# GpSimd builds the next state-space tile's tables between a pair's two tiles, ahead of the next tile's parameters

## What is computed

```
for i in range(DEPTH):                          # DEPTH 2, SEQ 256, D_MODEL 2048
    h = rmsnorm(x, norm_w[i])
    (u, s5_gate, z, xbc, dt_raw, q, k, v, att_gate,
     merge_logits) = jnp.split(h @ w_in[i], pts, axis=-1)
    y_s5  = s5_mixer(u, ...) * silu(s5_gate)        # diagonal complex state-space model
    y_ssd = ssd_mixer(z, xbc, dt_raw, ...)          # Mamba-2, 16 heads, chunks of 64
    y_att = window_attention(q, k, v, att_gate, ...)# 16 heads, window 128
    branches = einsum('bnw,nwd->bnd', [y_s5, y_ssd, y_att], w_branch[i])
    x = x + (sum_b sigmoid(merge_logits_b) * branches_b) @ w_out[i]
```

## Time and profile before

| | us |
|---|---|
| median of 3 runs | 1879.06 (1876.44 to 1883.75) |
| the profiled execution, its own time | 1878.58 |
| its span | 1876.9 |
| PE busy | 1826.9 (97%) |
| DVE busy | 1384.8 (74%) |
| ACT busy | 951.5 (51%) |
| POOL busy | 541.5 (29%) |

### The profile page before, as it was taken

One profiled execution on the slowest core, in us unless ns is written; L12 is line 12 of the kernel. 1 busy time (PEld: TensorE's weight loads), 2 busy tenths in 40 slices (PEclk: granted clock), 3 DMA queues, 4 the chain that ended last, 5 costly groups with the idle time before them and its releaser, 6 DMA issues.

```text
span 1876.9 us, 34933 instructions
## 1 busy us (share of the span) xinstructions
PE 1826.9 (97%) x11720; PEld 1555.7 (83%) x11720; DVE 1384.8 (74%) x1865; ACT 951.5 (51%) x1128; POOL 541.5 (29%) x632
## 2 busy tenths in 40 slices
PE   6999999999999999999999999999999999999998
PEld 5888888878787888888889888887777788888887
DVE  6986666888787777666588766678787876766656
ACT  5344444666657564434454344456656565533334
POOL 5053444163451010003412434433352600000044
PEclk9999999999999999999999999999999999999999
DMA  7455555556555547665555555555565555566655
GB/s 286 160 203 185 185 193 186 189 201 215 185 188 189 182 175 265 224 240 210 201 188 188 191 184 193 185 200 202 187 192 199 190 185 177 193 247 241 230 202 201
DMA packets 80786, 376.97 MB, mean 201 GB/s; under 512 B 20848, under 2 KB 27536, under 8 KB 41872
## 3 DMA queue, kind: packets, MB, share of 16 engines
q1 hardware_dynamic: 76560, 360.00, 54.5%
q0 software_dynamic: 2368, 10.99, 2.2%
q10 hardware_dynamic: 1760, 4.75, 0.6%
HBM read 356.00 MB, written 21.79 MB: 201 GB/s over the span
## 4 chain that ended last, share of the span: by engine, by line
PE 79%; DVE 8%; issue 6%; DMA 3%; ACT 3%; POOL 1%; DVEq 0%; SPq 0%; ACTq 0%; POOLq 0%
PE mm L1709 21%; PE mm L1740 12%; PE mm L1741 12%; PE mm L1742 12%; PE mm L1710 11%; DMA raw<-in_stream 2%; DVE w_lo L1035 2%; ACT w_hi L716 1%; PE mm L1693 1%; PE mm L1695 1%; PE mm L1694 1%; PE b L1852 1%; PE bs L1862 1%; POOL ssum L510 1%; PE bs L1868 1%
## 5 line engine op out<-in xcount | busy, mean ns | idle before, releaser
L1035 DVE TENSOR_TENSOR w_lo<-raw,w_hi 128x2048 fp32r<-128x2048 f32 x299 | 698.3, 2336 | 205.7 <-ACT w_hi L716 195.8
L716 ACT ACTIVATE w_hi<-raw 128x2048 fp32r<-128x2048 f32 x299 | 571.3, 1912 | 459.7 <-DMA raw<-in_stream 459.1
L1709 PE MATMUL mm<-h_both,w_hi 128*128 128x512 f32 x1792 | 636.7, 400 | 0.3 <-DVE h_both L1628 0.3
L1710 PE MATMUL mm<-h_both,w_lo 128*128 128x256 f32 x1792 | 503.2, 281 | 0.0
L1709 PEld LDWEIGHTS mm<-h_both,w_hi 128*128 128x128 f32 x1792 | 336.6, 188 | 84.9 <-DVE h_both L1628 1.0
L1710 PEld LDWEIGHTS mm<-h_both,w_lo 128*128 128x128 f32 x1792 | 338.5, 189 | 0.1
L1740 PE MATMUL mm<-w_lo,h_both 128*128 128x512 f32 x768 | 313.4, 408 | 0.0
L1741 PE MATMUL mm<-w_hi,h_both 128*128 128x512 f32 x768 | 301.0, 392 | 0.0
L1742 PE MATMUL mm<-w_hi,h_both 128*128 128x512 f32 x768 | 300.7, 391 | 0.0
L697 POOL TENSOR_TENSOR ssum<-ssum,proj 128x256 f32<-128x256 f32 x32 | 76.7, 2397 | 380.2 <-ACT proj L1004 353.2
L1740 PEld LDWEIGHTS mm<-w_lo,h_both 128*128 128x128 f32 x768 | 144.5, 188 | 33.9 <-issue 4.1
(11 more groups left out here) (335 smaller groups left out, 2591.0 us busy)
## 6 DMA issues: line engine op xcount, KB each, us to landing
raw<-in_stream SPq DMA_DIRECT2D x300, 1024.0 KB, 4.9
gscr<-gt SPq DMA_DIRECT2D x48, 256.0 KB, 5.9
gin<-gscr SPq DMA_DIRECT2D x24, 512.0 KB, 5.6
bd<-in_bdense SPq DMA_DIRECT2D x16, 384.0 KB, 5.2
lam<-lscr SPq DMA_DIRECT2D x128, 32.0 KB, 3.3
crow<-cscr POOLq DMA_DIRECT2D x16, 256.0 KB, 5.6
x_old<-out POOLq DMA_DIRECT2D x2, 2048.0 KB, 11.9
out<-proj ACTq DMA_DIRECT2D x8, 512.0 KB, 5.4
```

The lines of the kernel that those rows point to most:

```text
L716: e.activation(w_hi[:, j % RAW, :], raw[:, j % RAW, :], ACT.Copy).then_inc(hi_done, 1)
L1035: e.tensor_tensor(w_lo[:, j % RAW, :], raw[:, j % RAW, :], w_hi[:, j % RAW, :].bitcast(F32), ALU.subtract).then_inc(lo_done, 1)
L1709: e.matmul(mm[:, j % 2, :], w_hi[:, j % RAW, w], h_both[:, k].rearrange("p a t -> p (a t)"), start=k == 0, stop=False)
L1710: ins = e.matmul(mm[:, j % 2, 256:512], w_lo[:, j % RAW, w], h_hi[:, k, :], start=False, stop=k == KT - 1)
```

## The change

`s5_tile` is cut in two. `s5_table` holds its first part up to `bw3`, `s5_rest` the part from `dec` on. In the join stage both are called one after the other as before. In a pair `s5_table` is called first, behind a new wait for `yv` of the first tile of the previous pair (`t` 4, piece 4), and `parameters(0)` comes after it:

```
-            def s5_tile(L, I, more, between):
+            def s5_table(L, I, more):
 
                 W.s5(L, I, more)
                 i = I + more
...
                 SGp.mark(e.tensor_tensor(bw[:, 1, :], bw[:, 1, :], b2[:, 0, :], ALU.add), "bw3")
 
+            def s5_rest(L, I, more, between):
+
+                i = I + more
                 W.wait(SV, "wim", 1)
...
                 with e.Fori(0, 4) as I:
-                    s5_tile(L, I, 0, lambda: None)
+                    s5_table(L, I, 0)
+                    s5_rest(L, I, 0, lambda: None)
...
+                    W.tile(L, I, 0)
+                    W.wait(MV, "yv", 2)
+                    s5_table(L, I, 4)
                     parameters(0)
                     W.wait(MG, "cur4")
-                    s5_tile(L, I, 4, lambda: values(0))
+                    s5_rest(L, I, 4, lambda: values(0))
                     parameters(1)
                     values(1)
```

## The result

| us | before | after |
|---|---|---|
| median of 4 runs each | 1879.53 (1876.44 to 1883.75) | 1900.43 (1897.49 to 1904.63) |
| the profiled execution, its own time | 1878.58 | 1897.49 |
| its span | 1876.9 | 1895.8 |

The ratio is 1.0118 (95% interval 1.0100 to 1.0135): 1.2% slower, 20.9 us of the median and 18.9 us of the profiled span. The forecast was 1889, with a range up to 1899: the direction was right, the size half of what came, and the median lies 1.4 us above the range.

What follows compares the result with a forecast made beforehand. PE, busy almost throughout, was taken as the bound, so only its waits count: 1878.58 - 9.7 (wait for `pt`) + 19.8 (lateness at the gate) = 1888.7, say 1889 us. The 8-in-10 range was 1870 to 1899.

Steps and rivals of the forecast that it cites:

- The saving: Second tile, PE's product with `pt`: without tables there the 1.61 us wait goes, in six pairs 9.7 us less.
- The collision with the fifteen table instructions: First tile after `yv`: DVE's two-SBUF-input instructions alternate with GpSimd's tables, so the convolution ends 2.8 us later.
- `bw0` ahead of `xc`: Behind the convolution: `bw0`, released by the last `lam`, goes before `xc` and delays it by 1.29 us.
- and the `ex` one input; these I take as free: DVE's stretch up to `q_v`: `ex`, with one input, was assumed not to collide with GpSimd, so no time added.
- the rival of the small instructions: `bw1` to `bw3` also hold the six `ex`: `q_v` 6.2 us late, PE loses 32 us, 1901 us; chance 0.10.
- The gate: Piece 8: tanh ends 2.76 us after `q_v`, which is 4.1 us late; PE 3.3 us late, 19.8 us in six pairs.
- Its cover: Piece 8's second half: 1.04 us between tanh and PE, less 0.2 for semaphore and weight load, leaves 0.8 us.
- The wait for `xc`: PE's transpose of `xc` waits 1.8 us, counted within the 3.3 us of piece 8, not on top.
- the first pair of each layer, which I had costed at nothing: Its tables are made in the join stage and wait for `cos` and `lam` there anyway, so no cost.
- the DMA of `crow`, which I took as late and free: With `parameters(0)` some 10 us later than before, but needed only in the next pair, so costed at nothing.

Runs made afterwards that it cites:

- the four that keep its order on GpSimd: Changed kernel with: `yv` wait removed, 1868.05 us; tables behind `end`, 1876.70; ACT's gate ahead of log, 1873.01; nine filler matmuls on PE, 1894.22.
- the first experiment: Changed kernel with `bw0` to `bw3` moved behind `parameters(0)`, the fifteen table instructions left at `yv`: 1870.43 us, ratio 0.9957.
- The run of collisions: Kernel without the encoder, copying input to output; rows of ten DVE instructions per form beside idle GpSimd, products, memsets or copies; one-input form beside products 1310 ns.
- two small edits: Each on the changed kernel: `bw0` to `bw3` moved behind `parameters(0)`, 1870.43 us (0.9957); only the new wait for `yv` removed, 1868.05 us (0.9952).
- the kernel before with the gate ahead: Kernel before, with ACT's second-half tanh `gate(1, 1)` written ahead of log and exponential of `q_v`: 1879.54 us, ratio 1.0015.

## Why the prediction was right and wrong, step by step

- **The saving.** 1.61 us x 6 = 9.7 us, by PE's way from the transposes to `pt`: 2.12 us in all second tiles. Right.
- **The collision with the fifteen table instructions.** Expected 2.8 us; DVE's stretch between the two `w_lo` grew by 14.58 - 11.72 = 2.86 us. But DVE's first `w_lo` now stands 458.54 - 444.02 = 14.52 us ahead of PE's product, before 534.76 - 521.28 = 13.48 us: it starts 1.04 us earlier against PE, so only 1.8 us are late. I had assumed that DVE starts where it did, and that was the other side of the saving. In the trace of before the distance is 14.52 us in the first pair of each layer, which has no pair with tables ahead of it, and 13.2 to 13.5 us in five of the six others; the last pair of layer 1, behind the stretch at half clock, has 14.52 too. The tables in a second tile thus left DVE behind for the next pair. In the trace of after all eight pairs have 14.52.
- **`bw0` ahead of `xc`.** Expected 1.3 us, measured 1.52 - 0.42 = 1.10. Right, and the load of `lam` that lets it start came as the earlier trace rows said.
- **The step that failed: "and the `ex` one input; these I take as free".** They took 3.28 instead of 1.26 us, 2.0 us more, beside `bw1` to `bw3`. This was the rival of the small instructions, to which I gave 0.10; its 2.1 us (6.2 - 4.1) were the right size. `q_v` is late by 2.86 + 1.10 + 2.02 - 1.04 = 4.9 us, forecast 4.1. By the prediction's own sum these 2.0 us are worth 12 us in six pairs; DVE's earlier start, 6 us of luck, hid half of them.
- **The gate.** Tanh ends 2.76 us behind `q_v`, as forecast. Its cover was 4.94 - 3.95 = 1.0 us, forecast 0.8: the 0.2 us set aside for the semaphore and the weight load are not there, PE starts 0.05 us behind the tanh. PE loses 3.95 us per pair instead of 3.3, and 0.12 more in starting again (from there to the transposes 575.74 - 553.12 = 22.62 us, before 563.42 - 540.93 = 22.49). The wait for `xc` lies within it, as said, but is 0.55 us and not 1.8.
- **What had no term.** The half clock (three times some 1.5 us, less the 1.6 us that the kernel before lost in layer 1: +2.9 us), and the first pair of each layer, which I had costed at nothing: there the first tile waits for `xc`, 0.6 and 0.7 us, and PE's way between the two tiles' products with `rq` grows by 0.8 and 0.9, together +1.7. This is no collision. In that pair the DMA of `crow`, which I took as late and free, goes out early, at 320.32 instead of 338.65, beside a load of weights issued at 321.00; that load lands 7.8 us after its issue, before 4.9, ACT's `w_hi` waits 1.75 us for it, and `xc` comes late. In all five kernels whose `crow` goes out there (after, and the four that keep its order on GpSimd) the first tiles wait for `xc`, in the others they don't; in the first experiment it goes out at 304.90.

The sum by the runs is 6 x (3.95 + 0.12 - 1.61) = 14.8, + 2.9 + 1.7 = 19.4 us. From the first tile's product with `rq` to that of the next pair, the six pairs with tables took 484.5 us before and take 503.7 after, 19.2 us more; the span grew by 18.9. The forecast had 10.1, so the profiled execution lies 8.8 us above it: by these terms the gate has 3.9 of it (6 x 0.65), the clock 2.9, the first pairs 1.7 and the starting again 0.7, together 9.2. The median is 2.9 us above the profiled execution here, before 0.9 us: two of the four runs took 1902.9 and 1904.6 at a mean granted clock of 0.991 and 0.994, against 0.996 in the profile. That they have more half-clock stretches is likely, but no trace of them shows it.

The Trainium skill (SBUF — State Buffer, Who interferes with whom) would have given the failed step. It lists `tensor_scalar` among the instructions that can run in a mode which takes both of DVE's ports, and says that in that mode DVE contends with GpSimd, without the exception that it makes for two SBUF inputs, which don't contend with an instruction that only writes. The run of collisions agrees on each count: 1310 ns beside products, 3.44 us for eleven beside memsets, and 0.42 us beside memsets for two inputs. I used the half of the rule on two inputs and let the other half go; in the trace of before no `ex` was stretched (all 96 took 0.27 to 0.29 us). But a row beside those that I read could have warned me. The step between the Newton products has one input, in SBUF, and constants; here in a first tile, without tables, and in the second tile of the earlier trace rows, while GpSimd's L546 ran from 543.37 to 543.77:

```profile
501.31 0.29 DVE L1051 TENSOR_SCALAR rq<-rq 128x256 f32<-128x256 f32 x1
...
543.49 0.43 DVE L1051 TENSOR_SCALAR rq<-rq 128x256 f32<-128x256 f32 x1
```

It took 0.40 to 0.43 us in the six tiles with tables and 0.29 or 0.30 in the ten others. The same page's advice to keep the colliding engine off the critical path holds, with an addition from these runs: most of the cost came where DVE, late by the tables, met the four `bw`, whose start a DMA sets.

## What to carry to other kernels

When a block of GpSimd work is moved, list for each DVE instruction beside it not only whether it has two SBUF inputs but whether it is a one-input SBUF-to-SBUF form, which stands too; of the forms tried here only those with an input in PSUM stood beside nothing. Cut the block where its waits are: here the part that needs only SBUF may run early, the part released by a DMA falls wherever DVE happens to be, and either of two small edits made a kernel that beats both (0.9957 and 0.9952; 1866.84 us, ratio 0.9936, for both together). A DMA that is issued earlier can delay a load that was issued beside it. And where a queue has a tanh that PE needs behind work that a late engine feeds, the cover between them (here 1 us) is what the late engine may cost before PE pays.

## What the runs showed of the hardware that I had not expected

A wait of 2.98 us of PE was followed by 1.2 GHz in three of six places that are otherwise alike (1.5 us each), by 2.4 GHz in the other three; with 0.94 us of wait and filler matmuls in none of six. Shorter waits did it too: those for `pt`, 1.2 to 1.7 us, in one of six before, and at 1.7 us in two of six in the kernel before with the gate ahead. And the price of a collision didn't depend on how small DVE's instruction is: beside products 128 columns stood as long (1.31 us) as 256 (1.27 us); eight of the small ones went by while GpSimd did its eight products.
